# A hybrid encoder trunk on one core: attention scores in a PSUM bank of their own, later adaLN sums, and a repacked first mixer

## The reference

```python
shift, scale, gate = adaln(c, w_ada_mix[l], b_ada_mix[l])
u = x * (1.0 + scale) + shift
y = hybrid_mixer(u, w_in[l], ..., w_out[l], cos, sin)
x = layer_norm(DN_ALPHA * x + (1.0 + gate) * y, ln1_g[l], ln1_b[l])
shift, scale, gate = adaln(c, w_ada_ffn[l], b_ada_ffn[l])
u = x * (1.0 + scale) + shift
y = conv_gated_mlp(u, w_up[l], ffn_conv_w[l], ffn_conv_b[l], w_down[l])
x = layer_norm(DN_ALPHA * x + (1.0 + gate) * y, ln2_g[l], ln2_b[l])
```

## Time and profile before

| What | us |
|---|---|
| median of 3 runs (lowest, highest) | 2347.07 (2346.17, 2348.88) |
| the profiled execution | 2345.82 |
| its span on the core | 2344.0 |
| PE busy in the span | 2149.4 |
| DVE, ACT, POOL busy | 1259.8, 1016.5, 1246.5 |
| mean granted clock of TensorE | 0.958 of 2.4 GHz |

### The profile page before, as it was taken

How to read it: one execution, slowest core, us unless ns; L and a number is a source line. 1 busy time by engine, 2 the same in 40 slices (tenths; PEclk the granted TensorE clock), 3 DMA queues, 4 the chain that set the end, 5 groups by cost and what they waited for, 6 DMA issues and landing times.

```text
span 2344.0 us, 25886 instructions
## 1 busy us (share of the span) xinstructions
PE 2149.4 (92%) x9503; PEld 1730.6 (74%) x9503; DVE 1259.8 (54%) x1923; ACT 1016.5 (43%) x1754; POOL 1246.5 (53%) x716
## 2 busy tenths in 40 slices
PE   2899387999899999999889999999999999999995
PEld 2677165886688878877677888887777888888884
DVE  4578765767731365577653264577773254333233
ACT  1555145424653455423464455523353364433232
POOL 0576265446558665454537867445434666444443
PEclk7899687999999999999899999999999999999997
DMA  7454142333445333332335523332222333333321
GB/s 261 128 145 135 36 122 76 92 97 105 121 135 166 99 87 89 101 90 81 107 104 148 168 80 104 93 97 87 85 77 86 93 89 96 100 100 119 98 85 50
DMA packets 413770, 247.80 MB, mean 106 GB/s; under 512 B 44261, under 2 KB 388941, under 8 KB 412621
## 3 DMA queue, kind: packets, MB, share of 16 engines
q1 hardware_dynamic: 411424, 245.47, 35.4%
q10 hardware_dynamic: 2221, 0.68, 0.1%
HBM read 241.85 MB, written 4.26 MB: 105 GB/s over the span
## 4 chain that ended last, share of the span: by engine, by line
PE 68%; DVE 10%; POOL 8%; issue 8%; ACT 5%; DMA 1%; ACTq 0%; POOLq 0%; DVEq 0%
PE fg L675 22%; PE fg L677 21%; PE fg L676 21%; POOL w_lo L1458 3%; POOL ada_acc L1501 2%; DVE bank_c L1190 1%; ACT probs L951 1%; POOL ssum L1537 1%; POOL ssum L1508 1%; DVE st L1292 1%; DVE probs L1304 1%; POOL q L1487 1%; ACT tmp L866 1%; DVE first_acc L1129 1%; DVE st L1290 1%
## 5 line engine op out<-in xcount | busy, mean ns | idle before, releaser
L1458 POOL TENSOR_TENSOR w_lo<-raw,w_hi 128x1024 fp32r<-128x1024 f32 (+2 forms) x392 | 858.5, 2190 | 925.2 <-ACT w_hi L858 925.1
L675 PE MATMUL fg<-u_hi,w_hi 128*128 128x512 f32 x2112 | 855.4, 405 | 18.9 <-DVE u_lo L1168 6.5
L676 PE MATMUL fg<-u_lo,w_hi 128*128 128x512 f32 x2112 | 832.3, 394 | 0.0
L677 PE MATMUL fg<-u_hi,w_lo 128*128 128x512 f32 x2112 | 832.0, 394 | 0.0
L858 ACT ACTIVATE w_hi<-raw 128x1024 fp32r<-128x1024 f32 (+2 forms) x392 | 379.5, 968 | 423.9 <-PE fg L677 355.7
L675 PEld LDWEIGHTS fg<-u_hi,w_hi 128*128 128x128 f32 x2112 | 402.8, 191 | 126.2 <-issue 26.1
L676 PEld LDWEIGHTS fg<-u_lo,w_hi 128*128 128x128 f32 x2112 | 403.6, 191 | 88.7 <-issue 8.2
L677 PEld LDWEIGHTS fg<-u_hi,w_lo 128*128 128x128 f32 x2112 | 402.5, 191 | 86.4
L1408 DVE SCALAR_TENSOR_TENSOR x<-fg,mod,x 128x512 f32<-128x512 f32 x160 | 120.0, 750 | 369.7 <-PE fg L677 369.0
L1190 DVE SCALAR_TENSOR_TENSOR bank_c<-glu,par,bank_c 128x512 f32<-128x512 f32 x448 | 304.0, 748 | 0.1
L675 PE MATMUL fg<-h_hi,w_hi 128*128 128x512 f32 x704 | 281.4, 400 | 4.3 <-DVE h_lo L1440 4.3
(11 more groups left out here) (188 smaller groups left out, 1844.8 us busy)
## 6 DMA issues: line engine op xcount, KB each, us to landing
raw<-in_w_up_dram SPq DMA_DIRECT2D x176, 512.0 KB, 3.8
ada<-in_w_ada_ffn_dram SPq DMA_DIRECT2D x48, 512.0 KB, 4.5
raw<-in_w_down_dram SPq DMA_DIRECT2D x64, 384.0 KB, 3.4
raw<-in_w_in_dram SPq DMA_DIRECT2D x40, 512.0 KB, 3.8
raw<-in_w_down_dram SPq DMA_DIRECT2D x64, 320.0 KB, 3.0
ada<-in_w_ada_mix_dram SPq DMA_DIRECT2D x32, 512.0 KB, 4.6
first_ada<-in_w_ada_mix_dram SPq DMA_DIRECT2D x8, 1024.0 KB, 6.9
raw<-in_w_in_dram SPq DMA_DIRECT2D x32, 256.0 KB, 3.5
```

Of the source, the lines that this page charges most:

```text
L675: pe.matmul(out[:], hi[:, k, :], rhi, start=k == 0, stop=False)
L676: pe.matmul(out[:], hi[:, k, :], rlo, start=False, stop=False)
L677: ins = pe.matmul(out[:], lo[:, k, :], rhi, start=False, stop=k == nk - 1)
L1458: pool.tensor_tensor(w_lo[n % NRAW][:, 0:nk, :], raw[n % NRAW][:, 0:nk, :], w_hi[n % NHI][:, 0:nk, :].bitcast(F32), ALU.subtract).then_inc ...
```

## The change

Five things are done.

1. The bank bank_v becomes bank_s, for the scores of all mixers alone (apart from transposes at the start and the end). Rotations, both halves of the v turn and, in mixers 1 to 3, the weighted values go to bank_t, where the turned probabilities already are. In the first mixer the values go to fg2. The waits between scores and taps are gone.
2. Attention of mixers 1 to 3 takes one chunk per ug/uv pair, from 8 slabs after the first q on (mixer 1 from slab 44): pr(p-1), pv(p-2) at ug, sc(p), mx(p), tr(p-1) at uv, none on d slabs. Taps are planned afterwards, around it. The second mixer's rotations stand at slabs 37 to 41. The rotary add of q and k is a step of its own (rs), last on its slab.
3. adaLN: two accumulators by turns; as stands two slabs after the last quarter (before: at the next slab). The chunks are placed by a table; chunks 18 to 23 come at slabs 106 to 157 (before: 168 to 201), chunks 12 to 17 at 42 to 81 (before: 60 to 93).
4. The first mixer: two g/a pairs of the second mixer, not three, stand before the o slabs, so these are slabs 22 to 29. `early` gives slabs 0 to 21 budgets of 58 to 75 units. By the planner's own arithmetic, the taps of the first mixer end 5 to 8 per slab: tile 0 at slab 5, tile 1 at 11, tile 2 at 16, and tile 3 has 6, 6, 5, 6 and 8 taps at slabs 17 to 21. The x LayerNorm after it has its mean at 30, variance at 33 and spreading at 34 (before: 32, 34, 35). The centring is put before the last pr and pv steps. In mixers 1 to 3 the taps end at slabs 66, 177 and 275 (before: 59, 168 and 266), and the conv norm follows.
5. An o slab takes its attention k-tiles (4 to 7) first. At a uv slab, the first background step is put before h_lo only if the next slab is a ug. The mean's matmul uses ones, and the division is part of the centring (DVE) and of the first 1/sqrt step; the constants shrink by 2 x 128 columns.

The core of the diff:

```diff
-    slabs += head_slabs(0, 1, heads[:4]) + conv_slabs(0, 1, range(3)) + out_slabs(0, 0)
-    slabs += conv_slabs(0, 1, [3]) + head_slabs(0, 1, heads[4:])
+    slabs += head_slabs(0, 1, heads[:4]) + conv_slabs(0, 1, range(2)) + out_slabs(0, 0)
+    slabs += conv_slabs(0, 1, range(2, 4)) + head_slabs(0, 1, heads[4:])
...
-    fixed = {"ro": 14, "mx": 11, "pr": 11, "pv": 4, "cc": 7, ... "il": 7, "fold": 8, "hist": 0}
+    fixed = {"ro": 14, "mx": 13, "pr": 11, "pv": 5, "cc": 7, ... "il": 10, "xt": 7, "fold": 8, "hist": 0}
+    early = [62] * 5 + [58] * 4 + [64] * 5 + [75] * (POS["o", 0, 0, 0] - 14)
...
+    def space(n):
+        if n < len(early):
+            return early[n] - used[n] - (8 if SLABS[n][0] == "a" else 0)
+        return room.get(SLABS[n][0], 50) - used[n]
...
+    def attention(mi, n):
+        p = 0
+        while p < NCH + 2:
+            if SLABS[n][0] == "ug":
+                chunk_step(n, mi, ("pr", p - 1), ("pv", p - 2))
+                chunk_step(n + 1, mi, ("sc", p), ("mx", p), ("tr", p - 1))
+                p += 1
+            n += 1
+        return n
...
+    quarters = {4: 2, 5: 6, 6: 10, 7: 14, 8: 18, 9: 22, 10: 26, 11: (30, 31, 36, 37), 12: 42, 13: (46, 47, 56, 57), 14: 58,
+                15: 62, 16: 74, 17: 78, 18: 106, 19: 124, 20: 128, 21: 140, 22: 144, 23: 154}
+    for c, ns in quarters.items():
+        ns = range(ns, ns + QUARTERS) if isinstance(ns, int) else ns
+        for part, n in enumerate(ns):
+            put(n, "ad", c, part)
+        put(ns[-1] + 2, "as", c)
...
+    def beat(n, i):
+        chunk_step(n, 0, ("sc", i), ("pr", i - 1), ("mx", i), ("tr", i - 2), ("pv", i - 3))
+
+    first = 14
+    for n in range(first, wait):
+        beat(n, n - first)
     taps(0, 1, wait)
-    for i in range(NCH + 3):
-        if 14 + i >= wait:
-            beat(wait, 0, i)
-    conv_norm(0, (wait,) * 4)
+    beat(wait, wait - first)
+    put(wait, "cm", 0)
+    for k in range(CT):
+        put(wait, "cc", 0, k)
+    for i in range(wait - first + 1, NCH + 3):
+        beat(wait, i)
...
-    x_norm(0, wait + 9, DT, wait + 11, wait + 12, wait + 12, DT + 1)
+    x_norm(0, wait + 9, 4, wait + 12, wait + 13, 4)
+    rope(1, range(37, 42), (42, 43))
+    attention(1, 44)
     n = taps(1, wait + 1, NSLAB)
-    g2 = POS["o", 0, 1, 0] - 1
-    n = behind(1, n + 1, g2, rope, beat, conv_norm)
+    conv_norm(1, (n + 1, n + 4, n + 6, n + 12))
...
-        n = taps(mi, a0, NSLAB)
         rope(mi, range(h + 1, h + 6), (h + 6, h + 7))
-        behind(mi, n + 1, POS["o", l, b, 0] - 1, None, beat, conv_norm)
+        attention(mi, h + 8)
+        n = taps(mi, POS["a", l, b, 0], NSLAB)
+        conv_norm(mi, (n + 1, n + 4, n + 6, n + 12))
...
-        ada_acc = sb("ada_acc", [P, T])
+        ada_acc = [sb(f"ada_acc{i}", [P, T]) for i in range(2)]
...
-        bank_t, bank_v, bank_l = psum("bank_t"), psum("bank_v"), psum("bank_l")
-        sc_bank = [fg[2]] + [bank_c[0]] * 3
+        bank_t, bank_s, bank_l = psum("bank_t"), psum("bank_s"), psum("bank_l")
+        pv_bank = [fg[2]] + [bank_t] * 3
...
-                for k in range(nk):
+                order = [*range(CT, DT), *range(CT)] if kind == "o" else range(nk)
+                for k in order:
...
-                take("tv"[j % 2], rope_add, (QT + 2) * mi + (j + 1 if j < QT else QT + 2))
+                take("t", rope_add, (QT + 2) * mi + (j + 1 if j < QT else QT + 2))
...
                 if i == 0:
                     pe.wait_ge(rope_add, (QT + 2) * (mi + 1))
-                    if mi:
-                        pe.wait_ge(conv_step, (CONV_K + 1) * CT * (mi + 1))
-                else:
-                    pe.wait_ge(att_exp, (QT + 1) * (NCH * mi + i) - 1)
+                take("s", att_exp, (QT + 1) * (NCH * mi + i + 1) - 1)
...
-                take("v", alo, n + 1)
+                take("t" if mi else "f2", alo, n + 1)
...
-                        if mi >= 2 and j == 0:
-                            dve.wait_ge(att_exp, (QT + 1) * NCH * mi)
...
-                dve.tensor_tensor(xs(b, k), xs(b, k), bank_l[:], ALU.subtract).then_inc(xcenter, 1)
+                dve.scalar_tensor_tensor(out=xs(b, k), in0=bank_l[:], scalar=-1.0 / D, in1=xs(b, k),
+                                         op0=ALU.mult, op1=ALU.add).then_inc(xcenter, 1)
...
-                    for step in mine[0:1]:
-                        background(step)
-                    mine = mine[1:]
+                    if SLABS[n + 1][0] == "ug":
+                        for step in mine[0:1]:
+                            background(step)
+                        mine = mine[1:]
                     dve.wait_ge(gate_act, 5 * f + 5)
...
-                    pool.wait_ge(ada_sum, c - CHUNKS_BEFORE + 1)
-                    pool.tensor_tensor(ada_acc[:], rows[:, 0, :], rows[:, 1, :], ALU.add).then_inc(ada_add, 1)
+                    if c >= CHUNKS_BEFORE + 2:
+                        pool.wait_ge(ada_sum, c - CHUNKS_BEFORE)
+                    pool.tensor_tensor(acc[:], rows[:, 0, :], rows[:, 1, :], ALU.add).then_inc(ada_add, 1)
```

More of the change, by code:

```diff
@@ L159, in put, with chunk_step @@
         used[n] += fixed.get(step[0], 0)
[L161 to L171, removed]
+    def space(n):
+        if n < len(early):
+            return early[n] - used[n] - (8 if SLABS[n][0] == "a" else 0)
+        return room.get(SLABS[n][0], 50) - used[n]
+    def chunk_step(n, mi, *names):
+        for what, i in names:
+            if 0 <= i < NCH:
+                put(n, what, mi, i)
     def taps(mi, n, until):
@@ L229, in x_norm @@
                 put(n, "xl", xi, k - 1)
+    quarters = {4: 2, 5: 6, 6: 10, 7: 14, 8: 18, 9: 22, 10: 26, 11: (30, 31, 36, 37), 12: 42, 13: (46, 47, 56, 57), 14: 58,
[5 more added lines that the diff above has]
+        put(ns[-1] + 2, "as", c)
+    for n, what, i in ((12, "gate", 0), (28, "ss", 1), (40, "gate", 1), (70, "ss", 2), (100, "gate", 2), (148, "ss", 3),
+                       (165, "gate", 3)):
+        put(n, "fold", what, i)
     for t in range(TB, TT):
@@ L280, in plan @@
                 put(o + 4 + part, "cst", 3, part)
-        x_norm(NORM_NO["m", l, b], o + 8, 2, o + 14, o + 16, o + 16, 1)
+        x_norm(NORM_NO["m", l, b], o + 8, 2, o + 14, o + 16, 1)
         f = NORM_NO["f", (0, 1)[mi == 3], (1, 0)[mi == 3]]
-        x_norm(f, o + 27, 2, o + 33, o + 35, o + 35, 1)
+        x_norm(f, o + 27, 2, o + 33, o + 35, 1)
     for t in range(TB):
         put(346 + 2 * t, "tm", t)
[L286 to L301, removed]
-    i = 0
-    while i < NCH + 3:
-        if SLABS[n][0] in ("uv", "d") or n >= until:
-            beat(min(n, until), mi, i)
-            i += 1
-        n += 1
-    conv_norm(mi, (start, start + 3, start + 5, start + 12))
-    return n
+    for n in range(NSLAB):
+        for step in list(STEPS[n]):
+            if step[0] == "ro":
+                at(n, "rs", *step[1:])
 plan()
@@ L642, in x_to_features @@
                 for half in (0, 1):
-                    if banks[half] is bank_t or banks[half] is bank_v:
-                        take("tv"[half], x_evac[half], t + 1)
+                    if banks[half] is bank_t or banks[half] is bank_s:
+                        take("ts"[half], x_evac[half], t + 1)
                     transposes(banks[half], half, lambda k: stage_in[t % 4][:, k * P:(k + 1) * P]).then_inc(x_t_done, 1)
@@ L698, in x_stat @@
                     take("l", xsmall, SMALL * xi + 1)
-                    variance(ones_d).then_inc(xstat, 1)
+                    totals().then_inc(xstat, 1)
                 else:
@@ L712, in c_stat @@
                     take("l", csmall, SMALL * mi + 1)
-                    variance(ones_c).then_inc(cstat, 1)
+                    totals().then_inc(cstat, 1)
                 else:
@@ L817, in _ @@
                         for half in (0, 1):
-                            take("tv"[half], y_evac[half], t + 1)
-                            to_tokens(t, half, (bank_t, bank_v)[half])
+                            take("ts"[half], y_evac[half], t + 1)
+                            to_tokens(t, half, (bank_t, bank_s)[half])
             for what in ("xm", "xv", "xr"):
                 x_stat(what, NORM_NO["f", 1, 1])
-            banks = [fg[0], fg[1], fg[2], bank_c[0], bank_c[1], bank_t, bank_v, bank_l]
+            banks = [fg[0], fg[1], fg[2], bank_c[0], bank_c[1], bank_t, bank_s, bank_l]
             for t in range(TB, TT):
@@ L826, in _ @@
                     out = banks[2 * (t - TB) + half]
-                    if out is bank_t or out is bank_v or out is bank_l:
-                        take("t" if out is bank_t else "v" if out is bank_v else "l", y_evac[half], t + 1)
+                    if out is bank_t or out is bank_s or out is bank_l:
+                        take("t" if out is bank_t else "s" if out is bank_s else "l", y_evac[half], t + 1)
                     to_tokens(t, half, out)
```

133 lines of the change are left out of this document (64 added, 69 removed).

## The result

The changed kernel takes 2295.8 us (2295.3 to 2296.7, four runs), the kernel before on the same chip 2346.95 us (2346.2 to 2348.9, four runs): ratio 0.9776, 95% interval 0.9763 to 0.9789. That is 51 us less by the medians (53 by the ratio), where 79 were forecast. The time lies outside the forecast's own range (2256 to 2282) and just inside the wide one (2244 to 2298), close to rival (a), but the cause is another one, as the experiments show. In e3 and in e9 one of the four runs had a lower granted clock (5521 us at 0.41 and 2434 us at 0.84); the ratios are without them.

What follows compares the result with a forecast made beforehand. TensorE, busy for 92% of the span, was taken to bound the kernel, with 159 us of stall in stages the change touches. Gains 15 + 20 + 12 + 27 + 5 = 79 gave 2347.1 - 79 = 2268 us, range 2256 to 2282 (8 in 10: 2244 to 2298).

Steps and rivals of the forecast that it cites:

- rival (a): Packed slabs: DVE becomes the bound, so the gain is only 47 us, time 2300; chance 0.20.
- first mixer: Slabs 1 to 24: taps placed by slab 21, first output slab ends near 281; gain 15 us, bounds 5 and 35.
- output slabs and first x norm: Slabs 25 to 37: adaLN sums wait for nobody and six slabs lie beneath the norm; gain 20 us, bounds 10 and 29.
- second mixer: Attention no longer waits for the last tap; of 18.3 us stall 6 stay, gain 12 us.
- third: Third mixer: attention freed from the last tap; of 30.0 us stall 3 stay, gain 27 us.
- fourth: Fourth mixer: attention freed from the last tap; of 9.2 us stall 4 stay, gain 5 us.
- All three balance, and the end of slab 13 comes near 159: Slabs 5 to 13: DVE, POOL and TensorE each about 6 to 6.5 us per slab; end near 159 instead of 161.6.
- 6 us of jitter: Second mixer: just under 1 us per pair stays as stall where adaLN adds run beside 7 pairs.
- No slack beside adds: Later mixers' bank_t: a_lo ends some 6.9 us after the ug slab, the turn comes at 7.0; 1.6 slack without adds.
- rival (c): Later mixers: one bank_t for turns and values slows 24 chunks, two 2.4 us waits each, 115 us; 2383; chance 0.05.
- Rival (b): The budgets hold and DVE's waits for the value copy vanish under taps; gain 109 us, 2238; chance 0.14.
- The rule that was weighed: Second mixer: two-SBUF-input DVE and SBUF-reading POOL instructions exclude each other; 2.4 us per pair, 17 less gain, 2285.

Runs made afterwards that it cites:

- e3: The changed kernel with POOL doing a slab's rotary product ahead of that slab's adaLN adds; 2289.1 us, ratio 0.9736.
- e9: The kernel of e1 with DVE's value copy behind the taps instead of ahead of them in slabs 14 to 20; 2277.0 us, ratio 0.9683.
- e1: The changed kernel with rotations in two banks, bank_t and bank_s, by turns; 2279.4 us, ratio 0.9697.
- e10: The kernel of e1 plus e3's edit, ScalarE's u inputs ahead of its adaLN scaling, and the second mixer's conv norm later; 2270.4 us, ratio 0.9661.
- e7: The kernel before with the adaLN part alone (two accumulators, later sums, new chunk table, small constants); 2301.9 us, ratio 0.9799.
- e11: The kernel of e10 with e9's edit added; 2262.8 us, ratio 0.9629.
- e6: The changed kernel with adaLN chunks 12 to 17 moved to slabs 82 to 105, behind the second mixer's attention; 2295.8 us, ratio 0.9770.

## Why the prediction was right or wrong

| term | forecast, us | measured, us |
|---|---|---|
| first mixer | 15 | 9.5 (307.7 - 11.5 - 286.7) |
| output slabs and first x norm | 20 | 15.2 (14.3 by the boundaries, and a rotation of 0.9 now done there) |
| second mixer (stalls of slabs 38 to 83) | 12 | -6.4 (19.4 before, 25.8 after) |
| third | 27 | 27.3 |
| fourth | 5 | 5.5 |
| slabs 84 to 153 | 0 | -1.0 |

**The step that failed** is "All three balance, and the end of slab 13 comes near 159": it ended at 166.9. No engine was over its share there, as the sum had it. But all rotations had gone to one bank, and I looked at bank_t only for turns and values. Rotation, sine product, taps, add and next rotation form a chain that no engine's sum shows, 9.7, 8.6 and 10.8 us per turn instead of 6.3. e1 puts the end of slab 13 at 156.1 and the first output slab's end at 277.4, inside the 275 to 281 that were to be seen. At slabs 38 to 43, where rotations were taken to be free, 9.5 us were lost; a second bank gives back 3.9 of them, and so does POOL's product coming first (e3). By e1 the two banks give back 18.5 us of the 28 that are missing, 11 of them in slabs 10 to 13. The Trainium skill (Perfetto Trace Analysis, Optimizing Tensor Performance) wants independent matmul groups to go through different PSUM banks, so that DVE empties one beside the next; by that rule the step was to be looked at, and e1 agrees (37.2 us became 26.2).

**Second mixer.** The pairs are as foreseen: four in a row took 14.0 us each between 504 and 560 us (13.0 to 14 forecast), and a turn waited 0.7 us in them for a_lo. The 6 us of jitter were too many there (2.4 in slabs 44 to 66). What I left out is slabs 67 to 83. The 11.2 us of stall there were put down to the taps' coupling and should have gone; they became 13.9. There the conv norm's steps meet the last chunks and the adds. TensorE's turns after, in the middle of the pairs and at that place:

```profile
539.78 0.63 PE L761 MATMUL bank_t<-const,probs 128*128 128x128 f32 x4 [0.71 <-DVE u_lo L1318]
634.67 1.09 PE L761 MATMUL bank_t<-const,probs 128*128 128x128 f32 x4 [3.95 <-DVE u_lo L1318]
```

DVE ahead of the second:

```profile
628.30 0.76 DVE L1421 SCALAR_TENSOR_TENSOR fg<-gate,par,fg 128x512 f32<-128x512 f32 x1 [2.55 <-ACT fg L1042]
629.76 1.96 DVE L1306 TENSOR_TENSOR st<-st 128x4 f32<-128x4 f32 x1
631.97 1.62 DVE L1310 TENSOR_TENSOR probs<-probs,st 128x512 f32<-128x512 f32 x1
634.11 0.41 DVE L1318 TENSOR_TENSOR u_lo<-bank_t,u_hi 128x256 fp32r<-128x256 f32 x1
```

The a_lo stands behind everything that is late. "No slack beside adds" was right, and rival (c) named the mechanism; over all mixers it costs 6.9 us in six waits, not 115. That the norm's place is the cause is shown by e10: with a later norm the 11.4 us of e1 became 3.2.

**Third and fourth mixer**: right in size. But the third's 27 was put down to the bank, with two sums' waits as a part; e7 shows that moving and decoupling the adaLN sums gives 19.4 of it without any bank. That the total of this term came out right is luck in part.

**First mixer's end.** DVE needed less than I gave it: slabs 17 to 20 took 9.5 to 10.4 us each, not 11.4, and DVE was busy for 62.3 of the 80 us from 165 to 245 (78%), where near 90% was to be seen. So rival (a) is not what happened, though these slabs were still longer than TensorE's 7.5. Its time was right for another reason. The wait of 2.4 us per chunk was kept, as said, and e11 against e10 shows that it was worth 7.5. Rival (b) had that half right. The forecast's own steps behind slab 21 add up to 270.2, not 271, which changes nothing.

**The first x norm** ends as forecast: 9.8 us of stall in slabs 36 and 37, 10.0 before. From slab 23 to 37 the forecast left 0.5 + 23.3 - 10.2 = 13.6 us of stall, and 17.3 stayed. The granted clock can account for most of those 4 us: 0.96 over the 70.8 us of slabs 23 to 33 is 2.8 us of full speed. No run tried it.

**The rule that was weighed.** The scaling beside adds and without them, after and in e6, 498 (500) to 567 us:

```profile
L1194 DVE SCALAR_TENSOR_TENSOR bank_c<-glu,par,bank_c 128x512 f32<-128x512 f32 x20 | 14.0, 747 | 0.0
L1306 DVE TENSOR_TENSOR st<-st 128x4 f32<-128x4 f32 x5 | 8.8, 1754 | 0.0
L1310 DVE TENSOR_TENSOR probs<-probs,st 128x512 f32<-128x512 f32 x5 | 7.2, 1439 | 0.2
```

```profile
L1193 DVE SCALAR_TENSOR_TENSOR bank_c<-glu,par,bank_c 128x512 f32<-128x512 f32 x21 | 14.8, 750 | 0.0
L1305 DVE TENSOR_TENSOR st<-st 128x4 f32<-128x4 f32 x5 | 8.8, 1753 | 0.0
L1309 DVE TENSOR_TENSOR probs<-probs,st 128x512 f32<-128x512 f32 x5 | 3.5, 692 | 0.2
```

With the adds away the scaling takes 692 ns for 1439, and the tap, which reads PSUM for one of its inputs, does not move (747 and 750). That is what the Trainium skill (SBUF — State Buffer, on the shared port pair) has. The 17 us that the rule would have cost did not come: slabs 44 to 59 have 1.0 us of stall with the adds and 0.2 without (e6), since pairs had that much room.

## What to carry to other kernels

Adding up each engine's work per slab finds a bound; it doesn't find a loop. When a buffer that was two becomes one, follow one full turn through every engine that touches it, with what stands in each queue between, and compare that with the beat: here 8.6 to 10.8 us against 6.3, in slabs where no engine was over 80% busy. And test the parts of a change alone before crediting one: the part that looked like housekeeping gave 47 of the 53 us by itself, and the one with the bank, put on top of it, was 8 us on the wrong side. Two banks for the rotations then gave 18.5.
